# Down-projection weights laid out by column half, the last expert's low half scattered early, and the residual products moved four experts ahead

## The reference

```python
h = x2[tok] @ w_gu[e] + b_gu[e]                    # (rows, 2048)
g = jnp.minimum(h[:, :D_FF], SWIGLU_LIMIT)
u = jnp.clip(h[:, D_FF:], -SWIGLU_LIMIT, SWIGLU_LIMIT)
y = (u + 1.0) * (g * jax.nn.sigmoid(SWIGLU_ALPHA * g))
return y @ w_down[e] + b_down[e]                   # (rows, 1024)
...
y_rows = y_rows.reshape(n_rows, -1) * row_gate[:, None]
return jnp.zeros_like(x2).at[row_tok].add(y_rows)
...
h = layer_norm(DEEPNORM_ALPHA * h + ff, ln3_g[l], ln3_b[l])
```

## Time and profile before

| | us |
|---|---|
| median of 3 runs | 1149.04 (1148.79 to 1151.02) |
| the profiled execution, its own time | 1149.14 |
| its span | 1147.1 |
| TensorE busy | 1056.9 (92%) |
| VectorE, ScalarE, GpSimd busy | 425.3, 171.3, 63.2 |
| mean rate from memory over the span | 388 GB/s |
| mean granted clock of TensorE | 0.968 of full speed |

### The profile page before, as it was taken

How to read it: one execution, slowest core, us unless ns; L and a number is a source line. 1 busy time by engine, 2 the same in 40 slices (tenths; PEclk the granted TensorE clock), 3 DMA queues, 4 the chain that set the end, 5 groups by cost and what they waited for, 6 DMA issues and landing times.

```text
span 1147.1 us, 20099 instructions
## 1 busy us (share of the span) xinstructions
PE 1056.9 (92%) x8010; PEld 464.0 (40%) x8011; DVE 425.3 (37%) x1266; ACT 171.3 (15%) x383; POOL 63.2 (6%) x39
## 2 busy tenths in 40 slices
PE   9999999998999769999976669999979989998997
PEld 8876559643333223333321213333323333333333
DVE  2767577582432213333311113333313313333323
ACT  2142111221111001111100001111101111111112
POOL 0503370000000000000000000000000000000000
PEclk9999999999999889999987879999999999999999
DMA  9965256989999999999999999999999999999995
GB/s 331 368 227 183 99 193 249 379 317 430 434 427 432 433 431 433 432 428 435 431 432 433 427 436 430 431 434 430 434 431 428 435 429 432 430 429 433 430 428 241
DMA packets 36095, 445.34 MB, mean 388 GB/s; under 512 B 3872, under 2 KB 5152, under 8 KB 21120
## 3 DMA queue, kind: packets, MB, share of 16 engines
q1 hardware_dynamic: 33312, 439.85, 91.1%
q10 hardware_dynamic: 2752, 5.04, 1.4%
HBM read 443.84 MB, written 1.05 MB: 388 GB/s over the span
## 4 chain that ended last, share of the span: by engine, by line
PE 69%; DMA 23%; DVE 4%; another core or an unknown queue 2%; ACT 1%; issue 1%; SPq 0%; DVEq 0%; POOL 0%; POOLq 0%
PE bank L991 23%; DMA ring<-in_w_down 15%; PE bank L1016 13%; DMA ring<-in_w_gu 8%; PE bank L686 6%; PE bank L967 6%; PE bank L632 5%; PE bank L954 3%; PE bank L811 2%; PE bank L960 2%; PE bank L874 1%; PE bank L998 1%; PE bank L1004 1%; PE bank L1009 1%
## 5 line engine op out<-in xcount | busy, mean ns | idle before, releaser
L991 PE MATMUL bank<-ring,wk 128*32 128x512 f32 x3072 | 370.3, 633 | 65.3 <-DMA ring<-in_w_gu 65.3
L991 PEld LDWEIGHTS bank<-ring,wk 128*32 128x32 f32 x3072 | 104.2, 116 | 304.0 <-issue 265.6
L2001 DVE TENSOR_SCALAR wk<-bank 128x256 f32<-128x256 f32 x51 | 21.6, 424 | 538.8 <-PE bank L991 538.8
L1016 PE MATMUL bank<-ring,wk 128*32 128x512 f32 x1632 | 203.5, 597 | 8.9 <-DMA ring<-in_w_down 8.9
L967 PE MATMUL bank<-wk 64*128 64x512 f32 x416 | 103.3, 615 | 2.9 <-ACT wk L1407 2.9
L1016 PEld LDWEIGHTS bank<-ring,wk 128*32 128x32 f32 x1632 | 62.7, 109 | 77.8 <-issue 49.8
L1393 ACT ACTIVATE wk<-wk 128x256 f32<-128x256 f32 x51 | 21.2, 417 | 455.2 <-DVE wk L2001 455.2
L632 PE MATMUL bank<-ring 128*128 128x256 f32 x320 | 70.7, 381 | 0.0
L686 PE MATMUL bank<-ring 128*128 128x512 f32 x152 | 66.4, 593 | 0.0
L967 PEld LDWEIGHTS bank<-wk 64*128 64x128 f32 x416 | 35.8, 186 | 71.4 <-issue 64.1
L632 PEld LDWEIGHTS bank<-ring 128*128 128x128 f32 x320 | 60.2, 190 | 8.9 <-issue 0.8
(11 more groups left out here) (370 smaller groups left out, 881.2 us busy)
## 6 DMA issues: line engine op xcount, KB each, us to landing
ring<-in_w_gu SPq DMA_DIRECT2D x55, 4096.0 KB, 34.8
ring<-in_w_down SPq DMA_DIRECT2D x27, 4096.0 KB, 38.4
ring<-in_w_gu SPq DMA_DIRECT2D x18, 2048.0 KB, 13.8
ring<-in_w_down SPq DMA_DIRECT2D x9, 2048.0 KB, 11.8
ring<-in_w_in SPq DMA_DIRECT2D x4, 2048.0 KB, 19.2
ring<-in_w_ck SPq DMA_DIRECT2D x2, 2048.0 KB, 21.3
ring<-in_w_cv SPq DMA_DIRECT2D x2, 2048.0 KB, 17.3
ring<-in_w_cq SPq DMA_DIRECT2D x2, 2048.0 KB, 8.4
```

The lines of the kernel that those rows point to most:

```text
L991: ins = mm(hidden(bank, g), rows[:, kk, c, :], half_columns(w[:, kk, :], g), start=False, stop=2 * c + kk == KT - 1, skip_group_check=True)
L1016: ins = mm(strip(7, 2 * d + b), actT[:, b, 2 * c + gg, :], wd[:, gg, b, 512 * d:512 * d + 512], start=c == 0 and gg == 0 and b == 1, stop= ...
```

## The change

1. `w_down` is laid out by output column half: chunk 4 (`low`) has all four k groups for columns 0 to 511, chunk 5 (`high`) for columns 512 to 1023. Each pass now loops g over 0 to 3 and takes both chunks for each g (`down_both`); `chunk_used[4]` is counted up in the last g, not half way.
2. The last expert has a pass of its own (`last_expert_pass`): all low products into bank 7, then high products into bank 4. ScalarE copies the low half to `ysb_low` as soon as it is complete, and TensorE adds it to bank 0 ahead of the last two down groups, and to bank 2 behind them. The high half goes out as `ysb_high` and is scattered last. These four products use all 128 rows.
3. The last chunk's second half comes as two transfers of 0.5 MB (`quarter_landed`, and the unit's semaphore).
4. VectorE takes `bn_stats` of the low halves inside its last loop, of the high halves after it; one `centre` of tile 0 moves behind `newton`. VectorE also clears `ysb` in the last expert's passes. Its loop and ScalarE's are split at place 31.
5. `add_rows` moves from ahead of place 31 to ahead of place 28.

```diff
-                    sp.dma_start(slot_words(at + 1)[:, 0:half], src[:, SLOT:SLOT + half]).then_inc(half_landed, 16)
-                    sp.dma_start(slot_words(at + 1)[:, half:SLOT], src[:, SLOT + half:2 * SLOT]).then_inc(done, 16)
+                    cuts = (0, half, half + half // 2, SLOT)
+                    for lo, hi, landed in zip(cuts, cuts[1:], (half_landed, quarter_landed, done)):
+                        sp.dma_start(slot_words(at + 1)[:, lo:hi], src[:, SLOT + lo:SLOT + hi]).then_inc(landed, 16)
...
+            def scatter_half(t, d):
+                y = (ysb_low, ysb_high)[d]
+                mm(psum[2 * t + d][:], scatT[:, t * P:(t + 1) * P], y, start=False, stop=True, skip_group_check=True).then_inc(scattered, 1)
...
+            def down(words, g, d):
+                wd = words.rearrange("p (g b n) -> p g b n", g=GROUPS, b=2)
+                for b in range(2):
+                    ins = mm(strip(7, 2 * d + b), actT[:, b, g, :], wd[:, g, b, :], start=g == 0 and b == 1, stop=g == GROUPS - 1,
+                             skip_group_check=True)
+                if d == 0 and g == GROUPS - 1:
+                    ins.then_inc(chunk_used[4], 1)
+                return ins
...
+            def down_half(bank, words, g):
+                wd = words.rearrange("p (g b n) -> p g b n", g=GROUPS, b=2)
+                for b in range(2):
+                    f = 2 * (g % 2) + b
+                    ins = mm(strip(bank, f), actT[:, b, g, :], wd[:, g, b, :], start=g < 2 and f > 0, stop=g >= 2, skip_group_check=True)
                 return ins
...
+                open_half(7, 0)
+                open_half(4, 1).then_inc(bias_used, 1)
+                low, high = chunk(4), chunk(5)
+                for g in range(GROUPS):
+                    ins = down_half(7, low, g)
+                ins.then_inc(chunk_used[4], 1)
+                pe.wait_ge(xrows_ready, j + 2)
+                transpose_gathered()
+                pe.wait_ge(half_landed, 16)
+                down_half(4, high, 0)
+                down_half(4, high, 1)
+                pe.wait_ge(y_low, e + 1)
+                scatter_half(0, 0)
+                pe.wait_ge(quarter_landed, 16)
+                down_half(4, high, 2)
+                pe.wait_ge(unit_landed[u * UNITS_PER_EXPERT + 2], it * 16 + 16)
+                down_half(4, high, 3).then_inc(chunk_used[5], 1)
+                scatter_half(1, 0)
+                pe.wait_ge(y_ready, j + 2)
+                scatter_half(0, 1)
+                scatter_half(1, 1)
...
-            with pe.Fori(heavy_turn + 1, LOOPS - 1) as it:
+            with pe.Fori(heavy_turn + 1, LOOPS - 2) as it:
                 for u in range(UNROLL):
                     all_passes(it, u)
+            for t in range(TT):
+                for d in range(2):
+                    add_rows(t, d)
             for u in range(UNROLL):
-                if u == UNROLL - 1:
-                    for t in range(TT):
-                        for d in range(2):
-                            add_rows(t, d)
-                all_passes(LOOPS - 1, u, ending=u == UNROLL - 1)
...
+            with act_e.Fori(till_last, passes_till(N_EXP - 1, N_EXP + 2)) as j:
+                sigmoid(j)
+                gates(j)
+                act_e.wait_ge(gath_done, j + 2)
+                af(xrows, psum[6][:, 0:Q], ACT.Copy).then_inc(xrows_ready, 1)
+                act_e.wait_ge(chunk_used[4], j + 1)
+                af(ysb_low, psum[7][:], ACT.Copy).then_inc(y_low, 1)
+                act_e.wait_ge(xgT_done, j + 2)
+                af(wk[:, 0:2 * P], psum[5][:, 0:2 * P], ACT.Copy).then_inc(xg_ready, 1)
+                act_e.wait_ge(chunk_used[5], j + 1)
+                af(ysb_high, psum[4][:], ACT.Copy).then_inc(y_ready, 1)
...
+            with dve.Fori(till_last, passes_till(N_EXP - 1, N_EXP + 2)) as j:
+                one_pass(j, last=True)
+                before = dve.snap(spread, min_val=0, max_val=4 * SEQ // SLOTS)
+                for t in range(TT):
+                    dve.wait_ge(scattered, before + (t + 1))
+                    v.bn_stats(lst[:, t, 0, :], psum[2 * t][:])
...
             for t in range(TT):
-                for i in range(2):
-                    dve.wait_ge(scattered, 2 * t + i + 1)
-                    ins = v.bn_stats(lst[:, t, i, :], psum[2 * t + i][:])
-                link(ins)
+                dve.wait_ge(scattered, low_halves + (t + 1))
+                link(v.bn_stats(lst[:, t, 1, :], psum[2 * t + 1][:]))
...
-            for i in range(2):
-                centre(0, i).then_inc(weighted, 1)
+            centre(0, 0).then_inc(weighted, 1)
             dve.wait_ge(lnlog_ready, 2 * TT + TT)
             newton(lrs, lag[:, :, 1], 2, nwt[:, 8:10]).then_inc(scale_ready, 1)
+            centre(0, 1).then_inc(weighted, 1)
```

More of the change, by code:

```diff
@@ L961, in transpose_gathered, with scatter @@
                 ins.then_inc(xgT_done, 1)
-            def scatter(end=False):
+            def scatter():
                 for t in range(TT):
@@ L1071, in expert_pass @@
                 open_rows()
-                for c in range(2):
-                    if c == 1:
+                low, high = chunk(4), chunk(5)
+                for g in range(GROUPS):
+                    if g == 2:
                         pe.wait_ge(xrows_ready, j + 2)
                         transpose_gathered()
[L1076 to L1085, removed]
@@ L1086, in expert_pass, with last_expert_pass, chunk @@
-                pe.reg_add(passes, passes, 1)
+                    ins = down_both(low, high, g)
+                ins.then_inc(chunk_used[5], 1)
+                pe.reg_add(passes, passes, 1)
+            def last_expert_pass(it, u):
+                j = pe.snap(passes, min_val=0, max_val=MAX_PASSES)
+                e = pe.snap(ended, min_val=0, max_val=SEQ // SLOTS - 1)
+                def chunk(c):
+                    s = chunk_slot(u, c)
+                    if c < 2:
+                        if c == 0:
+                            pe.wait_ge(slot_landed[s], 16 * (front_loads[s] + 2))
+                            pe.wait_ge(unit_landed[u * UNITS_PER_EXPERT], it * 16 + 16)
+                    elif c % 2 == 0:
+                        pe.wait_ge(slot_landed[s], 16 * (front_loads[s] + 3))
+                    elif c == 3:
+                        pe.wait_ge(unit_landed[u * UNITS_PER_EXPERT + 1], it * 16 + 16)
+                    return slot_words(s)
+                pe.wait_ge(aT_ready, j + 1)
+                pe.wait_ge(osel_ready, j + 1)
+                pe.wait_ge(y_ready, j + 1)
+                open_hidden(4)
+                pe.wait_ge(xg_ready, j + 1)
+                for c in range(4):
+                    if c > 1:
+                        keep_warm(4)
+                    gate_and_up(4, xg, chunk(c), c).then_inc(chunk_used[c], 1)
+                pe.wait_ge(scT_ready, j + 1)
+                pe.wait_ge(hot_ready, j + 2)
+                scatter()
+                transpose_gates(j)
+                transpose_act(j)
+                gather()
+                pe.wait_ge(aT_ready, j + 2)
+                pe.wait_ge(scT_ready, j + 2)
+                pe.wait_ge(bdown_moved, 1)
+                open_half(7, 0)
+                open_half(4, 1).then_inc(bias_used, 1)
+                low, high = chunk(4), chunk(5)
+                for g in range(GROUPS):
+                    ins = down_half(7, low, g)
[15 more added lines that the diff above has]
+                scatter_half(1, 1)
+                pe.reg_add(passes, passes, 1)
+                pe.reg_add(ended, ended, 1)
@@ L2007, in one_pass @@
                 v.tensor_copy(actT, psum[4][:, 0:2 * P].rearrange("p (b g s) -> p b g s", b=2, g=GROUPS)).then_inc(aT_ready, 1)
+                if last:
+                    v.memset(ysb, 0.0)
                 dve.wait_ge(scT_done, j + 1)
```

62 lines of the change are left out of this document (32 added, 30 removed).

## The result

The changed kernel takes 1151.39 us (median of 14 runs, 1149.23 to 1153.32), the kernel before 1149.16 beside it (14 runs). The ratio is 1.0016, 95% interval 1.0009 to 1.0022. That is slower by about 2 us, within the 0.2% that I called the same, but above my range, which ended at 1150.9.

A forecast was written before the change was run, and what follows sets the result against it. The weight stream was taken to bound the kernel over the experts, followed by a serial tail of 12 to 15 us. Tail -0.95 plus TensorE +0.86 made -0.09, so 1149.0 us, range 1147.7 to 1150.9.

The forecast's parts named there:

- -0.95 for the tail: Behind the last down products: early scatter and early low `bn_stats` end the aggregates sooner, 0.95 us gained.
- +0.86 for TensorE: Place 31: a 4.2 us wait slows the first burst by 1.70 us; last down products end 0.86 us later.
- 0 for the stream: Weight transfers up to the last landing: later count and third transfer cost 0, last landing stays at 1132.3.
- Late release: Third or fourth expert: `chunk_used[4]` 2.3 us later, cover 2.8 us, price 0; as rival up to 2.3 each, 4%.
- The room ahead of the last landing: Last pass: the wait for chunk 3 (0.39 us) and 0.45 of the old 1.04 us wait absorb TensorE's lateness.
- the 1.70 I took: First burst of place 31: clock loss after a 4.2 us wait, 1.70 us from a range of 1.4 to 2.9.
- The list of times: Last pass without delay: low products from 1127.8, scatter to 1131.9, groups 2 and 3 from 1132.36, leaving 0.45 us.
- The residual's products: Eight products, 3.7 us, moved ahead of place 28: cost 0 there, become a wait of 4.16 us ahead of place 31.
- the first high `bn_stats`: Tail, VectorE: starts at E + 2.05, with E the end of the last down products.
- the moved `centre`: Tail: VectorE's work behind the aggregates is the same sum in another order; the move alone brings nothing.
- the clearing of `ysb`: VectorE, after `actT` is out: 0 to 0.7 us of work where over 2 us are free, cost 0.
- the third transfer: Last chunk's second half in two transfers: taken as 0, at most 0.1 us, last landing still 1132.3.

The follow-up runs named there:

- late count alone: Only the count of chunk 4 moved ahead of the last down products of a pass, in the kernel before: 1150.65 us, ratio 1.0012.
- four or eight warming products: Small TensorE filler products in the wait ahead of place 31's first products, in the changed kernel: four 1149.23 us (one run), eight 1150.66 us.
- release mended: Changed kernel, singly loaded `w_down` refilled by k group halves, chunk 4 counted half through the pass; residual's products left at place 28: 1151.07 us, ratio 1.0015.
- wait filled: Eight warming products in the wait ahead of place 31: changed kernel 1150.66 us; with `w_down` also refilled by k group halves 1148.33 us.
- rows back: Changed kernel with the residual's eight products moved back ahead of place 31: 1150.38 us, ratio 1.0007.
- both mended kernels: Changed kernel, `w_down` refilled by k group halves, with residual's products back ahead of place 31 (1148.73 us) or eight warming products in that wait (1148.33 us).
- three kernels with the old release: Kernel before; it with only the residual's products moved ahead of place 28, 1149.34 us; it with six warming products in the first pass, 1148.90 us.

## Why the prediction was wrong

In the profiled executions the forecast was -0.95 for the tail, +0.86 for TensorE and 0 for the stream. Measured were -1.07, +2.01 and +1.44. Two steps failed, and most of the stream's lag in this one execution was chance.

**Late release: the step that failed.** I wrote that a cover of 2.8 us hides the release 2.3 us later, that the cover "decides when less than nothing is left", and took a price of 0. The late count alone costs about 1.5 us in the old kernel, and with a cover of 3.0 us the changed kernel lost 0.5 at the fourth expert; covers of 1.5 to 1.7 lost 1.9 to 2.1. The rate falls before the transfer ahead has landed and recovers only well after the next issue. I had a row to see that something lies there: an output transfer of 256 KB, 0.6 us of bytes at 431 GB/s, takes 2.4 us from issue to landing. I also took one execution's cover for the cover, though the release hangs on down products that run behind a wait that costs the clock. The late release was in my list of rivals with 4%, with its place named rightly and its threshold wrong.

The Trainium skill (DMA: Bandwidth & Descriptors, Anatomy of one DMA) gives about 2 us of fixed cost for a transfer, from a fit to transfers issued by GpSimd; these are issued by SP. I weighed it against the spacing of transfers issued far ahead, where it does not show, in these runs either. It belongs where the queue runs low. Here a cover of 3.0 us, more than its figure, did not hide everything.

**The room ahead of the last landing: mis-sized.** I had 0.39 + 0.45 us of it. The 0.39 held, the 0.45 was not there. With four or eight warming products, so without a clock loss, the new pass ends 1.18 us behind the last landing, where the old one ended 1.11 behind it. With the loss of 2.32 us it ends 3.12 behind: 1.94 more, which is the loss less 0.39. The loss itself was also larger than the 1.70 I took (the mean of my rows was 2.04). The 0.45 did not follow from my own terms either: the old 1.04 us less 0.2 for the biases and 0.86 for the scatter leaves nothing. The list of times that gave it left the 0.2 out and counted each step at 0.86 us. The timeline has starts at 1133.77, 1134.76 and 1135.82, that is 0.99 and 1.06 for a step between a strip product and a full-array product, where strips behind strips come every 0.86 us (1.92 less 1.06). The early product thus fills the last of the room that used to absorb late arrivals. That is why the idle place 31 costs 2.1 to 2.7 us in the new last pass (release mended, wait idle against filled) and nothing that can be told in the old one.

**Chance.** Of the stream's 1.44 us in the profiled execution, 1.3 came from two transfers that slipped without a late release. The loss at the fourth expert had been made good by then. That the late release costs time in the median rests on the late count alone and on the kernels with the release mended, not on this profile, and that its 2.38 us are so near to the 2.2 between the medians is luck.

**Right.** The residual's products cost nothing at place 28 and the time they free turns into a wait of about 4 us; the clock falls there; the tail gains 1 us (0.95 forecast, 1.07 measured); the first high `bn_stats` starts at E + 1.96 (2.05 forecast); the moved `centre` and the clearing of `ysb` leave no trace. Nor does the third transfer in most executions, though in two of nine the last quarter landed 0.3 to 0.5 us late.

**Open.** The parts do not add. The ratios by release and by what stands ahead of place 31:

| | wait left idle | residual's products there | wait filled |
|---|---|---|---|
| late release | 1.0016 | 1.0007 | 1.0008 |
| release mended | 1.0015 | 0.9997 | 0.9997 |

The late release costs 0.10% where the clock at place 31 is kept and next to nothing where it is not. In medians this is 1.6 to 2.3 us and 0.3. The intervals, about 1 us to either side, may be all of it. The clock loss itself is not the same in every execution either, as the last section shows.

The traces show one reason why they need not add. Near 1000 us, behind the heavy expert, the queue runs low in every kernel, with a cover of 2.0 to 4.5 us. The kernel before issues a `w_down` 4.0 us ahead of the landing before it, and the transfer comes 1.3 us later than the usual distance. The changed kernel has a cover of 3.4 there and comes 0.8 late, the late count alone 2.3 and 2.0, the rows back 2.0 and 2.5. So a lag that arrives at this place is not carried on as it is: against the kernel before, 0.9 us become 0.2 in the changed kernel, and 2.2 become 1.1 with eight warming products, but 2.2 become 2.7 with the late count alone and 2.1 become 3.2 with the rows back. No run isolates this place.

## What to carry to other kernels

A refill is in time only if it is issued well ahead of the previous landing: here 4.4 us of cover still lost 0.5 us at one place, 5.4 lost nothing anywhere. Read the cover in several executions when the release hangs on an engine whose clock varies. Work taken out of a place where the engine has slack does not vanish but becomes idle time, and on TensorE that can cost more than the work did; filler products are a cheap test and a cheap cure. Filling the last wait ahead of a deadline trades robustness for a fixed gain, so an upstream delay that was free before is paid nearly in full afterwards. Here both mended kernels stay within 0.1% of the kernel before, and no kernel is clear of it on the faster side: a tail gain of 1 us is about all this change holds.

## What the runs showed of the hardware

- Waits for transfers ahead of a full burst in the new traces also drop the clock: 3.93 us gave 5.96, 4.23 gave 6.48, and 2.81 gave 5.34, where 3.64 is full speed. Two waits of 0.8 and 1.2 us with 2.3 us of products between them did not.
- The length of the wait alone does not decide it. In all 14 traces, 158 of 162 such bursts behind a wait of 3.25 us or more took 4.91 to 6.60 us, but four behind waits of 4.01 to 4.04 ran at full speed. Behind waits of 2.2 to 2.7 us, 13 of 29 ran at full speed and the others took 5.08 to 5.34. Behind waits of 1.0 to 1.6 all five did.
- From the first single reload to the landing near 383 us, the three kernels with the old release agree within 0.06 us (130.65, 130.62 and 130.59). The late count scatters it over 1.4 us (131.23 to 132.67), and in the traces this follows the time of the first expert's down products. A release that just misses turns a steady stream into one that varies with the clock.
